# Loads of the second expert matrices issued by ScalarE behind each group's last activation, in a two-layer diffusion backbone

## What is computed

```
logits = h @ w_r + b_r;  top_v, top_i = top_k(logits, 2);  gates = softmax(top_v)
for e in range(8):
    out = out + combine[:, e:e+1] * ((silu(h @ w1[e]) * (h @ w3[e])) @ w2[e])
```

## Time and profile before

| | us |
|---|---|
| median of three runs | 1505.75 (1504.0 to 1505.98) |
| the profiled execution | 1505.96 |
| its span, first to last instruction | 1504.1 |
| PE busy | 1384.2 (92%) |
| DVE busy | 527.6 (35%) |
| ACT busy | 398.8 (27%) |
| bytes moved by DMA, mean rate | 395.89 MB, 263 GB/s |

### The profile page before, as it was taken

The page is one execution under the profiler, slowest core; times in us unless marked ns, Lnnn a source line. Parts: engine busy times, 40 slices in busy tenths (PEclk is TensorE's granted clock), DMA queues, the critical chain, the costliest instruction groups (busy, mean ns, idle before and its releaser), DMA issues.

```text
span 1504.1 us, 25283 instructions
## 1 busy us (share of the span) xinstructions
PE 1384.2 (92%) x11087; PEld 820.5 (55%) x11087; DVE 527.6 (35%) x957; ACT 398.8 (27%) x701; POOL 4.1 (0%) x8
## 2 busy tenths in 40 slices
PE   6899889999999999989799999999978998799865
PEld 3788558888888888888585333333322332233221
DVE  2799885432322333579844102001100001001112
ACT  3422484522222222475652101011000000001001
POOL 0000000000000000000000000000000000000010
PEclk8899999999999999999998999999999999999998
DMA  9997903533131143510535799999999999999995
GB/s 351 377 334 273 349 2 112 169 112 109 60 111 57 68 156 113 168 57 1 196 142 219 276 391 407 408 408 407 408 406 409 406 409 408 407 409 405 409 403 216
DMA packets 147029, 395.89 MB, mean 263 GB/s; under 512 B 7488, under 2 KB 38752, under 8 KB 146912
## 3 DMA queue, kind: packets, MB, share of 16 engines
q1 hardware_dynamic: 144000, 388.86, 68.2%
q10 hardware_dynamic: 2336, 3.24, 0.6%
q0 software_dynamic: 576, 2.10, 0.3%
HBM read 390.76 MB, written 3.41 MB: 262 GB/s over the span
## 4 chain that ended last, share of the span: by engine, by line
PE 73%; DMA 15%; DVE 6%; SPq 4%; ACT 1%; issue 1%; DVEq 0%; ACTq 0%
PE bank L1160 20%; DMA weight_ring<-in_exp_w 13%; PE bank L1191 6%; PE bank L1009 5%; PE bank L1007 5%; PE bank L1008 5%; PE bank L730 4%; PE bank L731 4%; PE bank L732 4%; SPq L572 3%; PE bank L1016 3%; PE bank L1018 3%; PE bank L1017 3%; DMA weight_ring<-in_w_ada 2%; PE bank L676 2%; PE bank L1199 2%
## 5 line engine op out<-in xcount | busy, mean ns | idle before, releaser
L1160 PE MATMUL bank<-weight_ring,gathered 128*32 128x512 f32 (+1 forms) x3840 | 399.7, 567 | 41.9 <-DMA weight_ring<-in_exp_w 41.9
L1160 PEld LDWEIGHTS bank<-weight_ring,gathered 128*32 128x32 f32 x3840 | 126.2, 111 | 292.0 <-issue 291.2
L2240 DVE TENSOR_TENSOR scratch<-scratch,bank 64x512 f32<-64x512 f32 (+1 forms) x60 | 38.4, 640 | 408.0 <-ACT scratch L1657 405.5
L1191 PE MATMUL bank<-weight_ring,scratch 128*32 128x512 f32 x1360 | 163.4, 598 | 12.4 <-DMA weight_ring<-in_exp_w 12.2
L1009 PE MATMUL bank<-slot_halves,slot_halves 128*128 128x512 f32 x336 | 130.7, 389 | 0.0
L1008 PE MATMUL bank<-hT_halves,slot_halves 128*128 128x512 f32 x336 | 130.7, 389 | 0.0
L1007 PE MATMUL bank<-slot_halves 128*128 128x512 f32 x320 | 124.6, 389 | 0.0
L1843 DVE SCALAR_TENSOR_TENSOR weight_ring<-scratch,conv_weights,weight_ring 128x512 f32<-128x512 f32 (+1 forms) x207 | 121.2, 634 | 2.6 <-ACT weight_ring L1434 0.7
L731 PE MATMUL bank<-hT_halves,slot_halves 128*128 128x512 f32 (+1 forms) x352 | 122.1, 347 | 0.0
L730 PE MATMUL bank<-slot_halves,slot_halves 128*128 128x512 f32 (+1 forms) x284 | 105.8, 373 | 8.1 <-DVE slot_halves L1750 5.2
L1191 PEld LDWEIGHTS bank<-weight_ring,scratch 128*32 128x32 f32 x1360 | 43.4, 110 | 115.9 <-issue 88.0
(11 more groups left out here) (314 smaller groups left out, 1582.2 us busy)
## 6 DMA issues: line engine op xcount, KB each, us to landing
weight_ring<-in_exp_w SPq DMA_DIRECT2D x216, 1024.0 KB, 18.3
weight_ring<-in_w_ada SPq DMA_DIRECT2D x24, 2048.0 KB, 13.0
weight_ring<-in_exp_w SPq DMA_DIRECT2D x64, 768.0 KB, 15.8
weight_ring<-in_ffn_w SPq DMA_DIRECT2D x33, 1024.0 KB, 5.6
weight_ring<-in_w_in SPq DMA_DIRECT2D x8, 1024.0 KB, 11.6
weight_ring<-in_w_out SPq DMA_DIRECT2D x4, 2048.0 KB, 11.6
weight_ring<-in_w_in SPq DMA_DIRECT2D x2, 3072.0 KB, 15.4
expert_rows<-scratch ACTq DMA_DIRECT2D x14, 128.0 KB, 6.0
```

The source lines that it names most:

```text
L1160: i = mm(ps[BLOCK * job:BLOCK * (job + 1), 0:cw], gathered_block(e, k, b), w[:, kk, a * cw:(a + 1) * cw], start=(k == 0), stop=(k == KT - 1))
L1191: i = mm(bank[6][quarter, :], at01[:, c0:c0 + BLOCK], w2[:, i_, half * 512:(half + 1) * 512], start=(first and i_ == 0), stop=(last and i_ ...
```

## The change

The loads of second weights leave SP's program. ACT issues them itself, each group's behind that group's last activation (`second_weights(g)` right behind `gated(g)`), with the same wait on `unit_done`, the same places, semaphores and sources. SP issues the first weights alone. Numbers of units and PE's order stay. ACT loads the expert numbers of positions 1 to 7 for itself, as SP does. The function `of_expert` moves out, to be called by both.

```diff
@@ block.sync: expert_weights
-                def of_expert(name, e):
-                    return t[name][0, e] if e == 0 else t[name][0, bass.ds(expert[e], 1)].rearrange("a k n -> (a k) n")
...
-                            load(v, unit(v, w), of_expert(name, e).rearrange("(k p) n -> p k n", p=P)[
+                            load(v, unit(v, w), of_expert(name, e, expert).rearrange("(k p) n -> p k n", p=P)[
                                 :, 2 * p:2 * p + 2, j * 1024:j * 1024 + w])
-
-                def second(g):
-                    e, j = divmod(g, CH)
-                    for u in range(ROW_UNITS[j]):
-                        v = UNITS * r + Y_UNIT[g, u]
-                        f0 = j * 1024 + u * 256
-                        load(v, unit(v, D), of_expert("exp_w2", e)[f0:f0 + 256, :].rearrange("(q p) n -> p q n", p=P))
 
                 for g in range(NG):
                     first(g)
-                    if g:
-                        second(g - 1)
-                second(NG - 1)
@@ block.scalar: experts
+                expert = {}
+
+                def second_weights(g):
+                    e, j = divmod(g, CH)
+                    if e and j == 0:
+                        act.wait_ge(most_ready, 1)
+                        expert[e] = act.value_load(expert_at[0:1, e:e + 1], min_val=0, max_val=NE - 1)
+                    for u in range(ROW_UNITS[j]):
+                        v = UNITS * r + Y_UNIT[g, u]
+                        f0 = j * 1024 + u * 256
+                        act.wait_ge(unit_done, v - UNITS_HELD + 1)
+                        act.dma_start(unit(v, D), of_expert("exp_w2", e, expert)[f0:f0 + 256, :]
+                                      .rearrange("(q p) n -> p q n", p=P)).then_inc(unit_in[v % UNITS_HELD], 16)
+
...
                     gated(g)
+                    second_weights(g)
                 first_turned(NG - 1)
```

More of the change, by code:

```diff
@@ L544, in rounds, with of_expert @@
                 end(0, True)
+        def of_expert(name, e, expert):
+            return t[name][0, e] if e == 0 else t[name][0, bass.ds(expert[e], 1)].rearrange("a k n -> (a k) n")
         block = ctx.enter_context(nc.Block())
```

## The result

| | before | after |
|---|---|---|
| median us | 1504.98 (4 runs, 1504.0 to 1505.98) | 1518.42 (4 runs, 1516.63 to 1521.38) |
| ratio to before | | 1.0092, 95% interval 1.0076 to 1.0108 |
| profiled execution, span | 1505.96, 1504.1 | 1521.38, 1519.5 |

The change costs 13.4 us. It was forecast at 1516.7 us, 10.9 us more than before, within 1510.0 to 1523.5: direction, size and range held. Two terms of the sum were off in opposite directions, though, so the nearness of the number is in part luck, and what makes the tail long had been named only in part.

What follows compares the result with a forecast made beforehand. Transfers of expert weights, at 409 GB/s from about 892 us, were taken as the bound. The start's 7.0 us and the tail's 3.9, all else 0, made +10.9 us and a forecast of 1516.7 us, range 1510 to 1523.5.

Steps and rivals of the forecast that it cites:

- The bound: From about 892 us the transfers of expert weights set the pace, at a full rate of 409 GB/s.
- (a): SyncE's side: it loses 88 issues and their waits, but the next first weights can't start earlier; worth 0.
- (b): ScalarE's side: it gains 88 issues, their waits and seven loads of an expert number; worth 0.
- (c): Start of the stage: second weights of groups 0 and 1 issued later leave DMA engines idle; cost 7.0 us, bounds 1 and 12.
- (d): Middle, behind 892 us: the queue does not run dry, only the order of landing changes; worth 0 while DMA is the bound.
- (e): Tail: the last group's three second units are issued only after its last activation; own share 3.9 us, bounds 2 and 6.
- More bandwidth: Rival for the long full-rate stretch: two queues keep the DMA engines fuller, 1500 us at 420 GB/s; chance of faster 0.06.
- TensorE as the bound: Rival: late transfers at the start are absorbed and only a tail of 2 us is left, 1507 us; chance 0.09.
- A blocked ScalarE: Rival: a full queue holds ScalarE's issues, making gather copies late in groups 1, 2, 7, 8; 1524 to 1532 us, chance 0.10.
- 821 to 829 with next to no traffic: Sign for (c) at the start of the stage: almost no DMA traffic from 821 to 829 us.
- 838 to 858 at 409: Sign for (c) at the start of the stage: the DMA rate is 409 GB/s from 838 to 858 us.
- Last landing 7 us later through (c): Sign for (c) at the end: the last weight landing comes some 7 us later for that reason alone.

Runs made afterwards that it cites:

- ends_sync: Changed kernel with second weights of groups 0, 1, 2, 22 and 23 issued by SyncE again at their old places: 1504.8 us, ratio 1.0002 to before.
- start_sync: Changed kernel with second weights of groups 0, 1 and 2 issued by SyncE again at their old places: 1513.3 us, ratio 1.0057 to before.
- only_22_sync: Changed kernel with group 22's second weights alone given back to SyncE, behind group 23's first weights: 1508.4 us, ratio 1.0019 to before.
- end_sync: Changed kernel with second weights of groups 22 and 23 issued by SyncE again at their old places: 1508.9 us, ratio 1.0030 to before.
- later: Changed kernel with each group's second weights issued one step later, behind the next group's copies of turned activations: 1563.6 us, ratio 1.0396 to before.
- last_act: Only group 23's second weights issued by ScalarE, behind its last activation, all other groups' by SyncE: 1503.7 us, ratio 0.9990 to before.
- ahead: Changed kernel with ScalarE's second-weight issues placed ahead of the group's activations instead of behind them: 1523.1 us, ratio 1.0120 to before.

## Why the prediction was right or wrong

**The bound.** Right. The rate stayed flat at 407, no weight was added, and what was lost is time in which the DMA engines had nothing to do, plus work behind the last landing.

**(a) SyncE and (b) ScalarE, each 0.** Right. ScalarE's issues took 0.38 us at the median, and ends_sync, with 70 of the 88 still on it, is level with before. (For group 0 the four second units take the slots of its units one to four, as (c) has it, and not five to eight.)

**(c) The start, 7.0 us.** The mechanism was right, the size too large. The windows give 4.3 us, start_sync 5.1, and only_22_sync and end_sync, in which the start's part alone is left, 3.2 and 4.6. The step that failed is "some 6.4 us of the room stay empty (1 before, 5.4 behind)". It hung on the moment of issue: ScalarE was taken to issue when its last activation had ended, at 836.0 and 861.7; it issued from 834.6 and 859.6 on the clock of before. By the 4.3 us, the room left empty was 9.5 - (10.3 - 4.3) = 3.5 us. What is missing from 6.4, 2.9 us, is near the 3.5 us by which the two issues came earlier (1.4 and 2.1).

**(d) The middle, 0.** Right, and shown by ends_sync. First weights landed 5.6 us later than the median of before, and TensorE's waits for them grew from 41.9 to 60.0 us. What it said of catching up on second units that are already there held too: the waits for those fell from 15.2 to 1.4. The text called this harmless "as long as DMA is the bound", though, and that has two limits it did not see: a second step of delay costs 45 us (later), and at the end of the stage the order in which units land decides. Nor did the second units get the half of the bandwidth that the text gives them there: with the gathers beside them they had a third of the packets, and behind the gathers 192 GB/s against 66.

**(e) The tail's own share, 3.9 us.** Too small: start_sync, in which the tail's part is left, stands 8.9 us over before, and end_sync returned 9.5. By the trace of after three terms of the step were mis-sized, and a fourth a little the other way. "PE's last pair takes 2.8 us" measured 5.0, in a stretch with a granted clock of 0.56, that is at 1.2 GHz for most of it (+2.2). "2.5 + 3 x 2.56 = 10.2 us to the third landing" measured 12.1, from 1490.68 to 1502.78 (+1.9): the first landed after 5.0 us as worked out, the second after 8.4 (7.6), the third after 12.1. The 15.4 us behind the last landing measured 16.7 (+1.3), of which 0.9 in the sum of rows on TensorE (3.7 us instead of 2.8). The last activation and the issue, 0.7, took 0.2 (-0.5), as the issue did not wait for it. 3.9 + 4.9 = 8.8, which agrees with the runs. The step had the last first weights landing within 2 us of everything else, which is so (1485.3, and 1485.9 for the last of group 22's); it did not say that this, through group 22, is the cause, and that the late issue of group 23 costs something only because of it. last_act and only_22_sync show it.

Together: 4.3 + 8.8 = 13.1 us, against 13.4 between the medians and 13.0 between the two traces (15.4 between the spans, less 2.4). The forecast's 10.9 came near because one term was 2.7 too large and the other 4.9 too small: the mechanisms were right, the nearness of the sum was luck. The 2.4 us lie ahead of the first issue that the change moves; they are in the profiled execution's 1521.38, which is 3.0 over the median.

**The rivals.** More bandwidth: false, no stage of the table and no slice of the plateau is above 409. TensorE as the bound: false, the time followed the two holes, and ends_sync, with single waits of up to 5.0 us (4.3 before), is no slower. A blocked ScalarE: false, as (b) says; the one kernel in which ScalarE's order did hold issues back is ahead.

**The checks named.** 821 to 829 with next to no traffic: so (2 GB/s from 821 to 831.8). 838 to 858 at 409: 391. Last landing 7 us later through (c): 4. PE's waits near 5 us each, and more of them after small experts: longer, but 3.0 us on average (60.0 in 20) with the longest at 6.4, and fewer in all; where they fall is not shown here. Three issues just behind the last activation, an idle DMA of 3 to 5 us before their bytes: so, though for some 6.5 us (1485.9 to 1492.5). ScalarE's issues over 1 us each: no, 0.38 at the median, with single ones up to 1.5.

## What to carry to other kernels

Where one queue carried all weights, the order of issue was the order of landing (all 280 units in the trace of before), and what landed last was what is used last. Moving a part to a second queue kept the rate but gave up that order: ScalarE's unit issued at 1457.82 landed at 1470.0, SyncE's issued at 1454.74 at 1485.3. Units that are wanted first can land last, and work that used to be hidden under the last transfers is left over. When such a change is priced, ask of the end of the stage not only when the last byte lands but how much work still waits behind the first unit it holds up; in the middle a ring of 16 units hid the change's delay in 19 groups at no cost, and a second step of the same kind cost 45 us.

## What was not expected of the hardware

- ScalarE's DMA issues don't wait for the activations ahead of them in its program to end: issued at 862.02, with the three activations ahead of it starting at 862.30, 862.92 and 863.53.
- After waits of 4.8 to 5.3 us TensorE's pairs took 4.9 to 5.0 us instead of 2.8 (four rows in two kernels), at a granted clock of 0.56 in one of the stretches (1485.3 to 1490.6 in after); after waits of 2.7 and 3.3 us, 4.5; with the wait filled by spare matmuls, 2.76. A wait of 1.1 us had no such effect (2.79).
- The last three units, alone on ScalarE's queue, moved at 417 GB/s while all were in flight, no slower than seven in flight on one queue or on two. But the third landed 12.1 us behind the first issue, not 10.2: the last 0.15 MB came at a falling rate (269 to 23 GB/s in the slices from 1499.8 to 1501.2), and the landing is at 1502.78. Why the end is so slow is not known. Where the last first weights end, the rate is low as well: 200 to 235 GB/s from 1480.3 to 1483.5.
- With three queues at work, each got about the same number of packets (298 to 321 from 1463 to 1471 us), so what a queue moves depends on the size of its packets too.
